# Centred values, unit keys in PSUM and a head norm cut in pieces, in a two-block kernel on one Trainium2 core

## The chip, the cores and the metric

The kernel runs on one core of one Trainium2 chip. The metric is the device time of one execution in microseconds (us), the median of several runs. It was 1239.25 us before the change (3 runs, 1236.81 to 1241.57).

## The reference, cut to what matters

512 tokens of width 1024 pass an RWKV-7 layer, a differential attention layer and then a second block (short convolution and stick-breaking attention). The change touches the RWKV layer alone, up to the first tiles of its output projection. `rh`, `wh`, `kh`, `vh` and `ah` are r, the decay, k, v and a, split into 16 heads of 64:

```python
kk = (k * k_k).reshape(B, S, H, N)
kk = kk / jnp.maximum(jnp.sqrt(jnp.sum(kk * kk, axis=-1, keepdims=True)), 1e-12)
k = k * (1.0 + (a - 1.0) * k_a)
bh = kk * ah
def step(state, inp):
    r_t, w_t, k_t, v_t, kk_t, b_t = inp
    sa = jnp.einsum('bhij,bhj->bhi', state, kk_t)
    state = (state * w_t[:, :, None, :] - sa[..., None] * b_t[:, :, None, :]
             + v_t[..., None] * k_t[:, :, None, :])
    return state, jnp.einsum('bhij,bhj->bhi', state, r_t)
mean = jnp.mean(y, axis=-1, keepdims=True)
var = jnp.mean(jnp.square(y - mean), axis=-1, keepdims=True)
y = (y - mean) * lax.rsqrt(var + GN_EPS) * ln_w + ln_b
bonus = jnp.sum(rh * kh * r_k, axis=-1, keepdims=True) * vh
return ((y + bonus) * jax.nn.silu(gate)) @ w_out
```

## The kernel before, in words

Activations lie as 8 tiles of 128 channels by 512 tokens (`NT` is 8, `TOK` is 512). A large product runs in **slots** of one output tile each: 24 matmuls of 128x512, three for each of 8 input tiles, because every fp32 number is split into a high and a low part (`split_product`, L639). ScalarE makes a slot's high weights (`hi`, L1310), GpSimd its low weights (`low_part`, L558, two subtractions of 128x512), both in two buffers, so `hi` of a slot waits for the product two slots back. Each engine runs one long program in the order in which it is written by hand, and semaphores tie them together. A wait at the head of an engine's queue holds up all that stands behind it.

The RWKV layer has these phases.

**Key and receptance runs** (8 slots each, L781 to L838). In the receptance run VectorE works through one key tile after another (`elements`, L2046; `receptance`, L2064; `bonus_mul`, L2069) and adds the token mix of the value run (`mix_v`, L2075). `elements(j)` multiplies the key by the reciprocal norm of its head, which TensorE has spread from 32 rows to a bank (`kk_spread`, L798, `head_spread`, L734). The unit key is kept in SBUF (`T1`, L2044). `kk_spread(j)` waits for the first instruction of `elements(j-1)` only (L802). The rows of reciprocal norms are first parted into a high and a low part for the fast fp32r product: L1472 on ScalarE, L2042 on VectorE. TensorE's order in an iteration is slot, `kk_spread(j+1)`, then `block_a(j-1)` (L805), whose 32 products are sent to DRAM.

**Value and gate runs** (L853 to L871). After each value slot `turn_v` (L840) turns a value tile with four transposes and `bonus_spread` spreads the bonus rows. VectorE meanwhile inverts 64x64 triangular problems in 30 steps (L2121). The steps stand in one order with `bonus(j)` (L2109) and with `lo_mix` (L1985), the low parts of the gate run's input, whose high parts are ScalarE's (`split_mix`, L1386). ScalarE also stacks the turned values (`stack_v`, L1527) and writes the bonus to DRAM (`bonus_out`, L1535).

**Chunk loop** (`NC` is 8, L993 to L1014). The turned blocks leave through `TURNED` (L274, L2153) and come back by DMA. For each chunk of 64 tokens TensorE runs `w_of`, `u_of`, `y_state`, `s_of`, `y_chunk`, while GpSimd places keys and values (L575 to L591) and scales the state, and ScalarE keeps y (`keep_y`, L1607).

**Head norm** (L1016 to L1037). Only when all of y is there, 8 matmuls subtract the mean of each head (L1030), ScalarE squares (L1644), TensorE sums over heads (L731), ScalarE takes the root and VectorE parts it (L2235). TensorE spreads it (L1037), and VectorE scales, adds the bonus and splits tile after tile (L2291 to L2301) for the first slot of the output projection. The first residual tile is L2251.

```python
        for k in range(NT):
            if k + 4 < NT:
                gated_bonus(k + 4)
            if k + 2 < NT:
                gn_scale(k + 2)
            if k + 1 < NT:
                gn_add(k + 1)
            split_lo(A_RWO, 0, k, YT[:, k, :])
```

SyncE's queue issues the weights and most other loads in order (L375 to L509). The bonus comes back in one load of 2 MB behind the last y (L505 to L507).

Of the kernel before, what the change touches and what calls it, by code (L numbers as in the profile page):

```python
# [25 lines left out]
P = 128  # L26
# [35 lines left out]
for _name, _w in (("ident", P), ("ones", P), ("center", P), ("causal_add", P), ("strict_add", P),  # L62
                  ("strict_s", CH), ("incl_s", CH), ("head_pick", 2 * BL),
                  ("pick", 2 * BL), ("eps", 6)):
    CONST_COLS[_name] = (_at, _at + _w)
    _at += _w
# [3 lines left out]
def constant_tables():  # L70
# [13 lines left out]
    eps = np.concatenate([eps, np.where(low_part, -1.0, 1.0)[:, None], low_part[:, None]], axis=1)  # L84
# [93 lines left out]
def gn_tile_bank(j):  # L178

    return (0, 1, 2, 3, 4, 5, 7, 0)[j]  # L180


# [10 lines left out]
def emit(nc, ctx, a, out):  # L193
# [60 lines left out]
    def over(start, entries):  # L254
# [19 lines left out]
    (TURNED,) = phase([("turned", [P, BL * BL])], tail_at + BL * BL * 4)  # L274
# [7 lines left out]
    BVT, SPREADH2, SPREADHR2, RK2, RKS2, RKC2 = phase([  # L282
        ("bonus_v", [P, NT, TOK]), ("spread_heads2", [P, 2, P]), ("spread_heads2_r", [P, 2, P], F32R),
        ("gn_rstd", [P, TOK]), ("gn_signed", [P, TOK], F32R), ("gn_parts", [P, TOK], F32R)])

    (GSQ,) = phase([("gn_squares", [P, NT, TOK])], 2 * FULL)
# [42 lines left out]
    def gn_bank(j):  # L329
        return BANK[gn_tile_bank(j)]  # L330
# [45 lines left out]
    def _(sp):  # L376
# [125 lines left out]

        sp.wait_ge(sem("v_placed"), 2 * 2 * NC)
        sp.dma_start(XT[:, :, :], D_XT.rearrange("j p t -> p j t")).then_inc(sem("x_spilled"), 16)
        sp.wait_ge(sem("y_even"), 2 * NC)  # L505
        sp.wait_ge(sem("y_odd"), 2 * NC)
        sp.dma_start(BVT[:, :, :], D_BV.rearrange("j p t -> p j t")).then_inc(sem("gn_in"), 16)  # L507
        sp.dma_start(SPREADH2[:, :, :], a["spread_heads"]).then_inc(sem("gn_in"), 16)
# [48 lines left out]
    def _(pool):  # L557
# [45 lines left out]

        def scale_state(c):
# [5 lines left out]
        for par in range(2):  # L610
            pool.wait_ge(sem(f"a_out{par}"), 16 * 4 * (NT // 2))
        scale_nk(0)
# [6 lines left out]
        pool.wait_ge(sem("prob_in"), 48)  # L619
        place_v(in_uv, 1)  # L620
        for c in range(NC - 1):
            if c:
                scale_state(c)
            place_kt(c + 1)
            place_v(in_sv(c + 1), 2 * c + 2)
            if c == 0:
                low_part(RUN_RWO[0], 1)
# [3 lines left out]
            place_v(in_uv, 2 * c + 3)  # L631
        for u in range(2, 4):
# [5 lines left out]
    def _(pe):  # L638
# [188 lines left out]
        for j in range(NT):  # L827
# [3 lines left out]
            else:  # L831
                rw_slot(NT + j, (lambda: kk_spread(NT - 1)) if j == NT - 1 else None)
# [7 lines left out]
        def turn_v(j):  # L840
# [3 lines left out]
            turn_four(BANK[6 - 2 * (j % 2)], [TMP[:, j % 2, t * P:(t + 1) * P] for t in range(TT)]).then_inc(sem("v_turn_mm"), 1)  # L844
# [8 lines left out]
        for j in range(NT):  # L853
# [3 lines left out]
            if j == 1:  # L857
                bonus_sums(1)
                pe.wait_ge(sem("kk_unit"), NT)
# [101 lines left out]
        def y_at(h, j):  # L961

            return YB[h][(low, up)[(h + j) % 2]][:, tile_cols(j)]

        def y_state(c):
            if c:
                pe.wait_ge(sem("y_even"), 2 * c)
                pe.wait_ge(sem("y_odd"), 2 * c)
            else:
                pe.wait_ge(sem("x_kept"), 8)  # L970
            for j in range(NT):
                for h, hp in enumerate((low, up)):
                    pe.matmul(y_at(h, j), SVX[c % 2][hp, j, h, :], KRX[hp, 1, j, chunk(c)], start=(j < 2), stop=False,
                              skip_group_check=True)

        def y_chunk(c):
# [3 lines left out]
            for j in range(NT):  # L980
                for h in ((0, 1), (1, 0))[j % 2]:
                    m = pe.matmul(y_at(h, j), UV[:, j, h, :], XR[:, c % 2, j, h, :], start=False, stop=(j >= NT - 2),
                                  skip_group_check=True)
            m.then_inc(sem("yx_mm"), 1)

# [7 lines left out]
        for c in range(NC):  # L993
            more = c + 1 < NC
            w_of(c)
            if c == 0:
# [6 lines left out]
            y_state(c)  # L1003
# [11 lines left out]

        pe.wait_ge(sem("y_even"), 2 * NC)  # L1016
        pe.wait_ge(sem("y_odd"), 2 * NC)
        center = cst("center")

        def gn_sums(b):  # L1020
            pe.wait_ge(sem("gn_squared"), 4 * b + 4)
            for j in range(4 * b, 4 * b + 4):
                m = head_sum(BANK[6], GSQ[:, j, :], j)
# [1632 lines left out]
```

## Time and profile before

| what | value |
|---|---|
| median of 3 runs | 1239.25 us (1236.81 to 1241.57) |
| the profiled execution | 1243.05 us |
| its span | 1241.3 us |
| busy in the span | PE 1161.3 (94%), DVE 753.1 (61%), ACT 619.9 (50%), POOL 486.4 (39%) |
| receptance run | about 120 to 190 us of the span |
| value and gate runs | about 184 to 287 us |
| chunk loop | about 287 to 370 us |
| head norm, to the first residual tile | about 370 to 408 us |

PE is TensorE, PEld its weight loads, DVE VectorE, ACT ScalarE, POOL GpSimd, SP SyncE. Times in rows count from the start of the span. A row of a timeline gives the start, the time of the group, the engine, the line, the operation with output and inputs, the number of instructions and, in brackets, how long the engine had been idle and what it waited for. The profiled execution is 3.80 us longer than the median.

### The profile page before, as it was taken

The numbers are of one execution on the slowest core, as the hardware profiler recorded it, in microseconds if no ns is written. First come the engines' busy times: TensorE is split into PE (matmuls) and PEld (weight loads), VectorE is DVE, ScalarE is ACT, GpSimd is POOL, SyncE is SP. The second block draws the span as 40 slices with busy tenths as digits, with TensorE's granted clock in tenths as the row PEclk, the third lists the DMA queues.
The fourth block names the chain that finished last, engine by engine and source line by source line (L and its number), as shares of the span: only waits on it lengthen the run. The fifth ranks groups of instructions, "written<-read, shape, count | busy, mean of one in ns | idle before, by whom it ended". The sixth has DMA issues, their size and how long they took to land.

```text
span 1241.3 us, 19538 instructions
## 1 busy us (share of the span) xinstructions
PE 1161.3 (94%) x7570; PEld 897.6 (72%) x7570; DVE 753.1 (61%) x1179; ACT 619.9 (50%) x1034; POOL 486.4 (39%) x391
## 2 busy tenths in 40 slices
PE   5899899998886999899999998999999999999987
PEld 5666667787772787677777776877888888867766
DVE  4775997895458436466666655374285234657773
ACT  4666453634553446566556464364221244556655
POOL 1333334357650344333323343443444445532231
PEclk8999899999997899899999999999999999999999
DMA  7742244526213253212222222522333333322111
GB/s 237 248 123 63 58 119 122 166 87 159 51 60 117 67 179 88 83 52 69 68 69 68 68 69 71 166 85 76 95 102 88 99 102 92 95 68 69 51 35 68
DMA packets 198941, 119.49 MB, mean 96 GB/s; under 512 B 27773, under 2 KB 187206, under 8 KB 198598
## 3 DMA queue, kind: packets, MB, share of 16 engines
q1 hardware_dynamic: 196256, 115.95, 32.1%
q10 hardware_dynamic: 2598, 2.33, 0.6%
q8 instruction: 60, 0.98, 0.3%
q14 instruction: 27, 0.22, 0.1%
HBM read 103.06 MB, written 15.20 MB: 95 GB/s over the span
## 4 chain that ended last, share of the span: by engine, by line
PE 41%; issue 30%; POOL 13%; DVE 12%; ACT 2%; DMA 1%; POOLq 0%; SPq 0%; ACTq 0%; DVEq 0%
POOL b_w_lo L562 13%; PE banks L643 10%; PE banks L645 10%; PE banks L644 10%; DVE b_problems L2127 1%; DVE b_sum_squares L2125 1%; PE banks L1218 1%; DVE b_a_lo L1987 1%; PE banks L650 1%; PE banks L891 1%; DVE b_suffix L2576 1%; PE banks L1246 1%; PE banks L910 1%; PE banks L1030 1%; DVE b_sum_squares L2060 1%
## 5 line engine op out<-in xcount | busy, mean ns | idle before, releaser
L562 POOL TENSOR_TENSOR b_w_lo<-b_w_raw,b_w_hi 128x512 fp32r<-128x512 f32 x320 | 430.4, 1366 | 710.7 <-ACT b_w_hi L1316 710.5
L643 PE MATMUL banks<-b_a_lo,b_w_hi 128*128 128x512 f32 x1280 | 524.9, 410 | 24.2 <-DVE b_a_lo L2243 8.6
L645 PE MATMUL banks<-b_a_hi,b_w_lo 128*128 128x512 f32 x1280 | 505.9, 395 | 0.0
L644 PE MATMUL banks<-b_a_hi,b_w_hi 128*128 128x512 f32 x1280 | 505.3, 395 | 0.0
L643 PEld LDWEIGHTS banks<-b_a_lo,b_w_hi 128*128 128x128 f32 x1280 | 244.1, 191 | 103.4 <-issue 21.6
L1316 ACT ACTIVATE b_w_hi<-b_w_raw 128x1024 fp32r<-128x1024 f32 x160 | 168.8, 1055 | 248.3 <-PE banks L645 242.9
L645 PEld LDWEIGHTS banks<-b_a_hi,b_w_lo 128*128 128x128 f32 x1280 | 244.0, 191 | 54.0
L644 PEld LDWEIGHTS banks<-b_a_hi,b_w_hi 128*128 128x128 f32 x1280 | 244.5, 191 | 44.5
L1723 ACT ACTIVATE b_exps<-banks,b_stats 128x128 f32<-128x128 f32 (+3 forms) x64 | 33.2, 524 | 61.3 <-DVE b_stats L2366 61.3
L1657 ACT ACTIVATE b_a_hi<-b_x_t,b_params 128x512 fp32r<-128x512 f32 x48 | 34.0, 719 | 55.5 <-DVE b_x_t L2251 54.9
L2251 DVE TENSOR_TENSOR b_x_t<-b_x_t,banks 128x512 f32<-128x512 f32 x32 | 22.0, 687 | 60.8 <-PE banks L645 60.8
L2364 DVE TENSOR_TENSOR banks<-banks,b_consts 128x256 f32<-128x256 f32 x32 | 13.9, 433 | 50.4 <-PE banks L1097 49.0
L2245 DVE SCALAR_TENSOR_TENSOR b_a_lo<-b_x_t,b_params,b_a_hi 128x512 fp32r<-128x512 f32 x32 | 30.1, 954 | 21.3 <-ACT b_a_hi L1657 21.3
L1710 ACT ACTIVATE b_rope_tmp<-banks 32x512 f32<-32x512 f32 x64 | 37.7, 588 | 3.0 <-DVE b_dq_t L2340 2.1
L1125 PEld LDWEIGHTS banks<-b_att_t,b_dv_rows 128*128 128x128 f32 x160 | 20.3, 190 | 14.5 <-issue 13.6
L1097 PE MATMUL banks<-b_dk_t,b_dq_t 64*128 64x128 f32 (+3 forms) x128 | 26.2, 487 | 4.7 <-DVE b_dk_t L2340 4.7
L2572 DVE TENSOR_TENSOR_SCAN b_suffix<-b_consts,b_softplus 128x512 f32<-128x512 f32 (+3 forms) x32 | 29.4, 919 | 1.1
L2365 DVE TENSOR_REDUCE b_stats<-banks 128x2 f32<-128x256 f32 (+3 forms) x32 | 26.4, 825 | 1.1
L1125 PE MATMUL banks<-b_att_t,b_dv_rows 128*128 128x128 f32 x160 | 26.2, 295 | 0.0
L2283 DVE TENSOR_TENSOR banks<-banks,b_rstd 128x512 f32<-128x512 f32 x16 | 11.2, 698 | 24.6 <-PE banks L645 18.1
L2484 DVE TENSOR_TENSOR b_conv_u<-banks,b_rstd 128x512 f32<-128x512 f32 x8 | 5.5, 692 | 32.0 <-PE banks L645 27.8
L2127 DVE TENSOR_TENSOR b_problems<-b_problems,b_sum_squares 128x60 f32<-128x60 f32 (+14 forms) x30 | 23.1, 771 | 1.0
(314 smaller groups left out, 1508.6 us busy)
## 6 DMA issues: line engine op xcount, KB each, us to landing
b_w_raw<-rw_w_in SPq DMA_DIRECT2D x32, 512.0 KB, 4.3
b_w_raw<-da_w_in SPq DMA_DIRECT2D x32, 512.0 KB, 4.0
b_w_raw<-w_in_a SPq DMA_DIRECT2D x32, 512.0 KB, 4.0
b_w_raw<-pe_w_gate SPq DMA_DIRECT2D x16, 512.0 KB, 4.1
d_ple<-b_ple_out SPq DMA_DIRECT2D x16, 256.0 KB, 4.8
b_w_raw<-rw_w_out SPq DMA_DIRECT2D x8, 512.0 KB, 4.6
b_ple_in<-d_ple SPq DMA_DIRECT2D x2, 2048.0 KB, 10.2
b_w_raw<-da_w_out SPq DMA_DIRECT2D x8, 512.0 KB, 4.1
```

The costliest lines, as they stand in the source:

```text
L562: m = pool.tensor_tensor(WLO[:, u % 2, ks], WRAW[:, u, ks], WHI[:, u % 2, ks].bitcast(F32), ALU.subtract)
L643: pe.matmul(dst, hi, a_lo[:, k_act, :], start=first, stop=False)
L644: pe.matmul(dst, hi, a_hi[:, k_act, :], start=False, stop=False)
L645: return pe.matmul(dst, lo, a_hi[:, k_act, :], start=False, stop=last)
L1125: m = pe.matmul(BANK[7][:, q * P:(q + 1) * P], DV[:, t, j * P:(j + 1) * P], ATTT[:, s % 2, t * P:(t + 1) * P], start=(t == 0), stop=(t == q))
L1316: act.activation(WHI[:, g % 2], WRAW[:, g % 4], ACT.Copy).then_inc(sem("hi_done"), 1)
L1657: m = act.activation(ACTS[buf][0][:, k, :], src, ACT.Identity, scale=scale)
L1710: m = act.activation(RTMP[32 * (q ^ 1):32 * (q ^ 1) + 32, 0, :], BANK[(3 * j + which) % 3][32 * q:32 * q + 32, :], ACT.Copy)
L1723: act.activation(ES[:, s % 2, comp, 0:w], PS[:, 3 + comp, 0:w], ACT.Exp, bias=STAT[:, s % 2, 2 + comp:3 + comp], scale=QK_SCALE, accum_out ...
L2127: own.step(tt(blk[:, :, 0:n, n + 1:BL], blk[:, :, 0:n, n + 1:BL], outer, ALU.add))
L2245: m = stt(out=a_lo[:, k, :], in0=src, scalar=scale, in1=a_hi[:, k, :].bitcast(F32), op0=ALU.mult, op1=ALU.subtract)
L2572: own.step(dve.tensor_tensor_scan(suf[:, h, ::-1], ONES[:, 0:1].to_broadcast([P, w]), sp[:, h, ::-1], 0.0, ALU.mult, ALU.add))
```

## The change

All of it lies in the RWKV layer:

- **Unit keys in PSUM.** `T1` becomes bank 6, where the spread norms lie. `kk_spread(j)` therefore waits for the whole of `elements(j-1)`. The parted rows are gone: ScalarE writes the reciprocal roots (with a factor of 4 under the root, since each head's row stands twice) and the spread is one plain fp32 matmul. The last column of each decay chunk (`PC`) is computed by ScalarE instead of copied by VectorE.
- **Two value mixes** (tiles 0 and 1) are made before the scans, not in the receptance loop.
- **Centred values.** `turn_v` multiplies by the centring matrix in place of the identity, so that y has mean zero in each head. The 8 centring matmuls of the head norm are gone.
- **Turned blocks** lie in a weight buffer, `WRAW[:, 2]`. GpSimd's first `place_v(in_uv, 1)` no longer waits for the problems' DMA. `place_v(in_sv(1))` and the first state do.
- **Head norm in pieces.** Columns 0 to 383 of y are squared on ScalarE and summed on TensorE in the last two chunks, columns 384 to 447 and 448 to 511 after them. The last chunk's y goes to banks 0 and 1, and VectorE keeps half of it. `ln_b` is added by ScalarE in `bonus_out`, GpSimd multiplies the bonus of tiles 0 to 3 and 4 by the gate in the chunk loop, VectorE multiplies y of tiles 0 to 4 by the gate ahead. The norm's scaling, adding and gating are done in PSUM, and the spreads of tiles 4 to 7 stand among the products of the first output slot.

```diff
-    (TURNED,) = phase([("turned", [P, BL * BL])], tail_at + BL * BL * 4)
+    TURNED = WRAW[:, 2].rearrange("p k n -> p (k n)")
+    PREGATED = 5
+    GN_SPLIT = (NC - 2) * CH
...
+        sp.wait_ge(sem("u_mm"), 4)
+        for j in range(4):
+            load_bonus(j)
+        sp.wait_ge(sem("u_mm"), 6)
+        for j in range(4, 6):
+            load_bonus(j)
+        sp.wait_ge(sem("s_mm"), 6)
+        for j in range(6, NT):
+            load_bonus(j)
...
-        sp.dma_start(BVT[:, :, :], D_BV.rearrange("j p t -> p j t")).then_inc(sem("gn_in"), 16)
...
-        pool.wait_ge(sem("prob_in"), 48)
+        pool.wait_ge(sem("bonus_v"), NT)
         place_v(in_uv, 1)
...
             place_v(in_sv(c + 1), 2 * c + 2)
+            if c == NC - 3:
+                for j in range(3):
+                    gate_bonus(j)
+            if c == NC - 2:
+                gate_bonus(3)
...
         def kk_spread(j):
             if j == 0:
-                pe.wait_ge(sem("kk_rstd"), 4)
+                pe.wait_ge(sem("kk_rstd"), 2)
             else:
-                pe.wait_ge(sem("kk_unit"), j)
-            head_spread(BANK[6], SPREADHR, RKC, j).then_inc(sem("kk_bcast"), 1)
+                pe.wait_ge(sem("el_done"), j)
+            head_spread(BANK[6], SPREADH, ACC, j).then_inc(sem("kk_bcast"), 1)
...
-            turn_four(BANK[6 - 2 * (j % 2)], [TMP[:, j % 2, t * P:(t + 1) * P] for t in range(TT)]).then_inc(sem("v_turn_mm"), 1)
+            bank = BANK[6 - 2 * (j % 2)]
+            for t in range(TT):
+                m = pe.matmul(bank[:, t * P:(t + 1) * P], TMP[:, j % 2, t * P:(t + 1) * P], cst("center"), start=(t == 0),
+                              stop=(t == TT - 1), skip_group_check=True)
+            m.then_inc(sem("v_turn_mm"), 1)
...
             w_of(c)
+            if c == NC - 1:
+                y_state(c)
+                gn_sums(slice(0, GN_SPLIT), 4, range(4))
...
-            y_state(c)
+            if more:
+                y_state(c)
+            else:
+                gn_sums(slice(0, GN_SPLIT), NT, range(4, NT))
...
+        gn_sums(slice(GN_SPLIT, GN_SPLIT + CH), NT + 1)
...
+        gn_sums(slice(GN_SPLIT + CH, TOK), NT + 2)
...
+        def first_out_slot():
+
+            pe.wait_ge(sem("lo_done"), RUN_RWO[0] + 1)
+            pe.wait_ge(sem("bank_free"), RUN_RWO[1] - 3)
+            for k in range(NT):
+                pe.wait_ge(sem("act_ready"), A_RWO + k + 1)
+                last = split_product(BANK[0], RUN_RWO[0] % 2, lambda w, k=k: w[:, k, :], k, k == 0, k == NT - 1, 0)
+                if k + 4 < NT:
+                    gn_spread(k + 4)
+            last.then_inc(sem("mm_done"), 1)
...
-        act.activation(RKS[:, :], RK, ACT.Identity, scale=SIGN).then_inc(sem("kk_rstd"), 1)
+        own.step(act.activation(RK, RK, ACT.Ln, scale=4.0))
+        act.activation(ACC[:, :], RK, ACT.Exp, scale=-0.5).then_inc(sem("kk_rstd"), 1)
...
         def bonus_out(j):
             act.wait_ge(sem("bonus_v"), j + 1)
+            own.step(act.activation(TMP[:, 2 + j % 2, :], TMP[:, 2 + j % 2, :], ACT.Identity, bias=prm(LN_B, j)))
...
+            if c == NC - 2:
+                act.wait_ge(sem("x_mm"), 2 * NC)
...
+                for j in range(NT):
+                    gn_square(slice(0, GN_SPLIT), j)
...
-        T1, T3 = ACC[:, :], RB[:, :]
+        T1, T3 = BANK[6], RB[:, :]
...
+            if j >= 2:
+                mix_v(j)
...
-            if k + 4 < NT:
-                gated_bonus(k + 4)
             if k + 2 < NT:
                 gn_scale(k + 2)
             if k + 1 < NT:
                 gn_add(k + 1)
-            split_lo(A_RWO, 0, k, YT[:, k, :])
+            split_lo(A_RWO, 0, k, BANK[4 + k % 4])
+            if PREGATED <= k + 1 < NT:
+                gn_gate(k + 1)
```

## Rows read from the trace of the kernel before

**Rows 1.** The page's chain that ended last, share of the span by engine.

```profile
PE 41%; issue 30%; POOL 13%; DVE 12%; ACT 2%; DMA 1%; POOLq 0%; SPq 0%; ACTq 0%; DVEq 0%
```

**Rows 2.** Timeline of ScalarE, then VectorE, before the first spread.

```profile
124.53 0.72 ACT L1472 ACTIVATE b_head_signed<-b_sigmoids,b_consts 128x512 fp32r<-128x512 f32 x1
...
125.28 0.75 DVE L2042 SCALAR_TENSOR_TENSOR b_head_parts<-b_sigmoids,b_consts,b_head_signed 128x512 fp32r<-128x512 f32 x1 [2.11 <-ACT b_head_signed L1472]
```

**Rows 3.** Timeline of VectorE in the receptance run.

```profile
143.30 0.74 DVE L2051 SCALAR_TENSOR_TENSOR b_sum_squares<-b_kt_rt,b_params,banks 128x512 f32<-128x512 f32 x1
...
145.35 1.27 DVE L2058 COPY b_kt_rt<-b_sum_squares 128x8 f32<-128x8 f32 x1
...
146.65 1.73 DVE L2060 SCALAR_TENSOR_TENSOR b_sum_squares<-b_sum_squares,b_nb_kh 128x512 f32<-128x512 f32 x1
...
178.52 0.74 DVE L2051 SCALAR_TENSOR_TENSOR b_sum_squares<-b_kt_rt,b_params,banks 128x512 f32<-128x512 f32 x1
...
183.82 6.48 DVE L1987 TENSOR_TENSOR b_a_lo<-b_mix_v,b_a_hi 128x512 fp32r<-128x512 f32 x7
```

**Rows 4.** Timeline of GpSimd, then VectorE, where the two overlap.

```profile
144.85 2.98 POOL L562 TENSOR_TENSOR b_w_lo<-b_w_raw,b_w_hi 128x512 fp32r<-128x512 f32 x2 [4.07 <-ACT b_w_hi L1316]
...
241.43 2.65 POOL L562 TENSOR_TENSOR b_w_lo<-b_w_raw,b_w_hi 128x512 fp32r<-128x512 f32 x2 [4.59 <-ACT b_w_hi L1316]
...
241.60 0.68 DVE L2114 TENSOR_TENSOR b_rw_tmp<-b_rw_tmp,banks 128x512 f32<-128x512 f32 x1
```

**Rows 5.** Timeline of TensorE in the receptance run.

```profile
128.21 0.80 PE L643 MATMUL banks<-b_a_lo,b_w_hi 128*128 128x512 f32 x1
...
136.25 0.49 PE L738 MATMUL banks<-b_head_parts,b_spread_heads_r 32*128 32x512 f32 x1
...
136.67 0.69 PE L815 MATMUL banks<-b_kt_rt,b_nb_kh 64*64 64x64 f32 x32
...
137.30 0.50 PE L643 MATMUL banks<-b_a_lo,b_w_hi 128*128 128x512 f32 x1
```

**Rows 6.** Windows: busy PE, PEld, DVE, ACT, POOL (instructions), PE clock, DMA share, GB/s.

```profile
124.00:128.00 4.00, 1.34 (x4) 0.46 (x2) 2.06 (x4) 3.97 (x8) 0.00 (x0) 0.81 0.17 52
...
128.00:132.00 4.00, 4.00 (x10) 3.02 (x10) 3.90 (x6) 0.98 (x2) 2.94 (x2) 0.50 0.02 4
```

**Rows 7.** Timeline of TensorE: plain fp32 products elsewhere.

```profile
104.24 1.13 PE L772 MATMUL banks<-b_lora_t,b_lora_w 64*128 64x512 f32 x4
...
1079.66 1.16 PE L663 MATMUL banks<-b_consts,b_params 128*128 128x128 f32 x8 [0.85 <-DVE b_params L1958]
```

**Rows 8.** Timeline of TensorE, ScalarE and VectorE, end of the value run.

```profile
232.51 0.60 PE L650 MATMUL banks<-b_consts,b_rw_tmp 128*128 128x128 f32 x4
...
239.03 0.60 PE L650 MATMUL banks<-b_consts,b_rw_tmp 128*128 128x128 f32 x4
...
239.55 0.49 PE L738 MATMUL banks<-b_head_parts,b_spread_heads_r 32*128 32x512 f32 x1
...
236.66 3.75 ACT L1395 ACTIVATE b_a_hi<-b_h_t 128x512 fp32r<-128x512 f32 x7
...
245.16 0.69 DVE L1987 TENSOR_TENSOR b_a_lo<-b_h_t,b_a_hi 128x512 fp32r<-128x512 f32 x1 [2.88 <-ACT b_a_hi L1395]
```

**Rows 9.** Timeline of TensorE, the first work on the turned blocks.

```profile
290.15 1.20 PE L925 MATMUL banks<-b_blocks_turned,b_blocks 32*32 32x32 f32 x64 [0.57 <-DMA b_blocks<-d_t]
```

**Rows 10.** Timeline of ScalarE, TensorE and VectorE in the head norm.

```profile
370.15 1.58 ACT L1582 ACTIVATE b_y_t<-banks 64x256 f32<-64x256 f32 x4 [1.37 <-PE banks L982]
...
371.88 7.94 PE L1030 MATMUL banks<-b_y_t,b_consts 128*128 128x512 f32 x14 [1.76 <-ACT b_y_t L1582]
...
387.24 0.80 PE L738 MATMUL banks<-b_gn_parts,b_spread_heads_r 32*128 32x512 f32 x4 [3.62 <-DVE b_gn_parts L2235]
...
388.04 1.28 DVE L2225 TENSOR_TENSOR b_y_t<-b_y_t,banks 128x512 f32<-128x512 f32 x2 [0.94 <-PE banks L738]
...
408.26 0.69 DVE L2251 TENSOR_TENSOR b_x_t<-b_x_t,banks 128x512 f32<-128x512 f32 x1 [2.38 <-PE banks L645]
```

More of the change, by code:

```diff
@@ L831, in _ @@
             else:
-                rw_slot(NT + j, (lambda: kk_spread(NT - 1)) if j == NT - 1 else None)
+                rw_slot(NT + j)
+            if j == NT - 1:
+                kk_spread(j)
             if j < NT - 2:
@@ L981, in y_chunk, with gn_sums @@
                 for h in ((0, 1), (1, 0))[j % 2]:
-                    m = pe.matmul(y_at(h, j), UV[:, j, h, :], XR[:, c % 2, j, h, :], start=False, stop=(j >= NT - 2),
+                    m = pe.matmul(y_at(c, h, j), UV[:, j, h, :], XR[:, c % 2, j, h, :], start=False, stop=(j >= NT - 2),
                                   skip_group_check=True)
             m.then_inc(sem("yx_mm"), 1)
+        def gn_sums(cols, squares, tiles=range(NT)):
+            pe.wait_ge(sem("rows_kept"), 6 * (NC - 1))
+            pe.wait_ge(sem("gn_squared"), squares)
+            for j in tiles:
+                m = head_sum(BANK[2][:, cols], GSQ[:, j, cols], j)
+            m.then_inc(sem("gn_mm"), 1)
         for g in range(2):
@@ L1058, in run_of @@
                 whole_slot(run, j, a0, buf, norm[1] if norm is not None and j == 1 else None)
-        run_of(RUN_RWO, A_RWO, 0)
+        first_out_slot()
+        for j in range(1, NT):
+            whole_slot(RUN_RWO, j, A_RWO, 0)
         run_of(RUN_PE0, A_PE0, 1, norm=norm_rows(16, 4))
@@ L1605, in keep_second_corner, with gn_square @@
             keep(dst[:, :, :, BL:CH], BANK[4 - h][block_rows(h, 0)].rearrange("p (n j t) -> p n j t", j=NT, t=BL), "corner_kept")
+        def gn_square(dst_cols, tiles):
+            act.activation(GSQ[:, tiles, dst_cols], YT[:, tiles, dst_cols], ACT.Square).then_inc(sem("gn_squared"), 1)
         def keep_y(c):
             act.wait_ge(sem("yx_mm"), c + 1)
-            for h, done in enumerate(("y_even", "y_odd")):
+            for h, done in enumerate(("y_even", "y_odd")[:1 if c == NC - 1 else 2]):
                 for par in range(2):
-                    src = BANK[6 + h][(low, up)[(h + par) % 2]].rearrange("p (j e t) -> p e j t", e=2, t=CH)
+                    src = BANK[h if c == NC - 1 else 6 + h][(low, up)[(h + par) % 2]].rearrange("p (j e t) -> p e j t", e=2, t=CH)
                     keep(YT[(low, up)[h], par::2, c * CH:(c + 1) * CH], src[:, par], done)
@@ L2017, in _ @@
             mixed(NKX[:, 1, k, :], MU_R, k).then_inc(sem("mix_done"), 1)
+        for j in range(2):
+            mix_v(j)
         dve.wait_ge(sem("tables_in"), 32)
@@ L2188, in keep, with gate_product @@
             dve.tensor_copy(dst, src).then_inc(sem(done), 1)
+        def gate_product(j, cols):
+            dve.wait_ge(sem("gn_squared"), j + 1 if cols.stop == GN_SPLIT else NT + 2)
+            own.step(stt(out=YT[:, j, cols], in0=YT[:, j, cols], scalar=prm(LN_W, j), in1=GT[:, j, cols], op0=ALU.mult, op1=ALU.mult))
         for g in range(2):
@@ L2205, in _ @@
                 keep_incl(c + 1, 0)
-            dve.wait_ge(sem("u_mm"), c + 1)
+            if c < NC - 1:
+                dve.wait_ge(sem("u_mm"), c + 1)
             if c == 0:
                 dve.wait_ge(sem("v_placed"), 4)
+            if c == NC - 1:
+                gate_product(0, slice(0, GN_SPLIT))
+                gate_product(1, slice(0, GN_SPLIT))
+                dve.wait_ge(sem("u_mm"), c + 1)
             keep(UV[up, :, 1, :], tiles(BANK[3][up]), "u_kept")
+            if c == NC - 1:
+                for j in range(2, PREGATED):
+                    gate_product(j, slice(0, GN_SPLIT))
             if c + 1 < NC:
```

147 lines of the change are left out of this document (75 added, 72 removed).

## The prediction, made before the changed kernel was run

> **What bounds the kernel now.** I read the page's chain first: TensorE has 41% of it, waits that the profile cannot name 30%, GpSimd 13%, VectorE 12% [rows 1]. That is an average. The change touches 120 to 408 us only, so I followed the timelines there.
>
> In the receptance run VectorE is the bound. From the first instruction of `elements(2)` at 143.30 to that of `elements(6)` at 178.52 its timeline has no gap: 35.2 us for four tiles, two extra mixes and one extra receptance (2.0 us together), so 8.3 a tile. The reader should see which durations are odd there: a copy of 8 columns takes 1.27 us, a 512-column multiplication 1.73 instead of 0.74 [rows 3], just while GpSimd makes low weights from 144.85 on [rows 4]. Each of GpSimd's two subtractions holds one such instruction up by about 1.05 us, 2.1 a tile. Undisturbed, a tile is 6.2. The multiplication at 241.60 reads one operand from a bank, lies wholly under GpSimd's row of 241.43, and takes 0.68 [rows 4].
>
> In the value run TensorE works without a gap, one slot in 6.52 us (232.51 to 239.03), of which 0.52 is `turn_v` and 0.42 the spread [rows 5, 8], so 5.58 is the slot. After it VectorE's inversion stands behind the last `lo_mix`, which at 245.16 had waited 2.88 for ScalarE [rows 8]. It ends the phase, through a DMA wait at 290.15 [rows 9]. In the head norm nothing overlaps: y is kept at 370.15, centring runs 7.94 us, the spreads start at 387.24, VectorE's tile loop at 388.04, and the first residual tile comes at 408.26, 2.38 after VectorE fell idle [rows 10].
>
> **The sum, part by part.** Negative is faster.
>
> *Start of the receptance run.* The parting of rows leaves the chain: 0.72 on ScalarE and 0.75 on VectorE, 124.53 to 126.03 [rows 2]. A plain fp32 spread comes in for a fast one. Two such products side by side take 1.13, with 1.06 to the next slot [rows 7], so I take 0.96 for one, against 0.42 between the starts of 136.25 and 136.67 [rows 5]. `elements(0)` starts 1.0 earlier. The bounds are -1.5 and -0.4.
>
> *The wait for all of `elements`.* `kk_spread(1)` now waits until `elements(0)` ends, near 131, not 127.5. Slot 9 is queued behind it, and its products are what receptance(1) needs. TensorE had already idled here: it was busy 1.34 of 4 us, and the granted clock went to 0.50 (1.2 GHz) in the next window [rows 6]. Slot 9 took 8.0 us at mixed clocks, 128.21 to 136.25 [rows 5]. After a longer idle I let it run 3.6 us at half speed again. It ends at 139.9, 3.7 later than before. The bounds are +1 and +6.
>
> *The pace after that.* TensorE needs slot 5.58, spread 0.96 and `block_a` 0.63 (136.67 to 137.30 [rows 5]), 7.2 a tile. VectorE loses the small copy and, with `T1` in a bank, most instructions with two SBUF inputs. Four are left (K times PI, the last product, mix and bonus). I give them one stall: 6.1 + 1.05 = 7.2. Both are at 7.2 against 8.3. Slot 14 ends at 139.9 + 5 x 7.2 + 1.0 (bonus sums) = 176.9. receptance(6), ahead of `elements(6)` on VectorE, waits for that, so `elements(6)` starts at 177.5 instead of 178.52 and, with one stall less, ends 1.6 before 183.82 [rows 3]. The value run starts its low parts **1.5 earlier**. The pace is worth 6 us and TensorE's new order takes most of it back. The two mixes ahead fill a VectorE that later waits for sigmoids, so cost nothing. With that cover gone they cost 2 x 0.74. ScalarE's small exponentials replace a copy, on an engine busy 0.98 of 4 us in its window [rows 6].
>
> Here a page of the Trainium skill bears. "SBUF — State Buffer", section "Who interferes with whom", says that a VectorE instruction with two SBUF inputs contends with a GpSimd instruction that reads SBUF, that one with at most one SBUF input does not, and that the loser waits. By that rule, the trace agrees (1.73 and 0.68 above). The same rule speaks against the full gain, since four such instructions stay.
>
> *The value run.* `turn_v` becomes four real fp32 products of 128 columns. The nearest row is four of that shape from 1079.66, 0.92 to the next matmul [rows 7], against 0.52: +0.4. Six of them lie before the last value slot has fed the gate run: **+2.4**. The bounds are 0 and +4.
>
> *`ln_b` on ScalarE.* An extra 128x512 instruction, 0.72 as in [rows 2], and a wait for it. Queued behind it are the splits of the gate run: once ahead of the seven splits from 236.66, once between `stack_v(5)` and the last split, for which the `lo_mix` at 245.16 waits [rows 8]. That puts two on the path: **+1.5**, bounds 0 and +1.7. Less 0.4 of slack in the first: net +1.1. The bonus DMA leaves some 2.4 us later, hidden in the 6.5 of a slot.
>
> So the chunk loop starts 1.5 earlier, then later by 2.4 and 1.1: **+2.0**. The new wait before `TURNED` is for a gate slot's low weights, done some 5 us before, and costs nothing.
>
> *The chunk loop.* GpSimd's placing of values is freed from a DMA. TensorE's wait there is not named by the trace, so 0, bounds -2.8 and 0. The bonus now comes during the loop, 2 MB in 8 loads, on SyncE's queue behind the turned blocks and ahead of x and the next weights. I take 0, bounds 0 and +3: TensorE's own instructions come by DMA too. GpSimd's gate products, 1.3 to 1.5 each [rows 4], are three ahead of one `place_v`; the same engine has a gap of 3 us at that point. Cost 0, at worst +1.3.
>
> *The head norm.* Half the sums of 384 columns and `y_state` stand ahead of the last `u_of`: +0.5, so y is ready at 370.65. VectorE finishes three gate products first, then copies its half: 372.0. Square 0.65, short sums 0.6, two ScalarE steps of 0.7: 374.65. The four spreads take 0.80 at half speed now [rows 10]. Plain fp32 doubles that: 376.4. VectorE's loop starts at **376.4 instead of 388.04**. It has 27 instructions at 0.61 (8 scale, 8 add, 8 low, 3 gate) for 28 before: 16.5. The last two low parts wait for ScalarE, +1.0. Spreads 4 to 7 stand in TensorE's queue behind products that wait for low parts. The first two at half speed are late by 2.2 together. End 396.1, then three products: residual at 397.2 against 408.26, **-11.0**. Bounds: -12.5 without late spreads, -7.5 if the clock stays at 0.50 (3.0 a tile on TensorE for 1.8 on VectorE).
>
> *Sum:* +2.0 - 11.0 = **-9.0**. The profiled execution's own 1243.05 would become 1234.05. It stands 3.80 above the median, so the median 1239.25 becomes **1230.3**. No later phase reads anything that moved, so I let the gain pass through.
>
> **The rivals.** A change under 0.5% (6.2 us) cannot be told from none by a measurement of this kernel.
>
> *A: the sum,* 0.38, own range 1226 to 1233.
>
> *B: the receptance run gains more,* 0.22. `elements(0)` has no stall and the clock comes back sooner, so slot 9 ends near 136.5 and both remaining terms shrink: 3.5 more. 1226.8. For it: GpSimd's pair falls within 3 us of a slot's end, where few two-input instructions stand. Against: the waits of the old order show only with TensorE already late.
>
> *C: the norm's loop becomes TensorE's,* 0.18. The clock stays at 0.50 and the norm gives -7.5: 1233.8. For it: TensorE has little to do between 370 and 380 now too, and the spreads from 387.24 take 0.80 instead of 0.5.
>
> *D: the stalls stay,* 0.13. Both of GpSimd's subtractions find a two-input instruction in each tile. The pace stays 8.3, costing 6 x 1.1 = 6.6: 1236.9. It is the same rule of the Trainium skill ("SBUF — State Buffer", "Who interferes with whom") taken to its end.
>
> *E: slower,* 0.09. The place is `kk_spread(j+1)`'s new wait. If `elements` ends about 2 us after the slot, TensorE idles and its clock falls again, as [rows 6] show after one idle. A slot at half speed costs 24 x 0.2 = 4.7 more. From three such slots on it decides: -9.0 + 14.1 = +5.1, 1244.4. Against it, my estimate has `elements` 0.5 us ahead of the slot.
>
> **How the numbers follow.** The forecast is A's 1230.3. The range 1223.5 to 1240 takes in B with the lower bounds, C and D, and leaves E and the ends out. Faster by over 0.5% means under 1233.05: A nearly whole, B, a third of C, 0.65. Slower over 1245.4: half of E and some sums of upper bounds, 0.08. Within: 0.27.
>
> **What would show it.** `elements(6)` should start near 177.5 and value slots be 6.9 apart. The turned blocks should be used near 292. Then VectorE's first scaling should follow the last y products by 6 us, not 18, and the first residual tile come 27 us after them, not 38. The 8-column copy should be short wherever it stands. I am wrong if TensorE's clock is 0.50 in several windows of 140 to 180, if nameless waits grow in the chunk loop, or if the low weights, not the norm, end the first output slots.

## The result, and the profile of the changed kernel

The changed kernel took 1246.62 us, the median of 13 runs (1243.35 to 1247.92), beside 1241.6 us for the kernel before (13 runs, 1236.81 to 1244.3). The ratio is 1.0045, 95% interval 1.0032 to 1.0059: 0.3 to 0.6% slower, where 1230.3 and a gain had been forecast. The profiled execution took 1247.3, its span is 1245.5, 4.2 longer than the span before.

The chain of the page, shares of the span by engine, answers to [rows 1]:

```profile
PE 47%; issue 29%; POOL 13%; DVE 6%; ACT 3%; DMA 1%; POOLq 0%; ACTq 0%; DVEq 0%
```

VectorE's share has halved, as the change wants, and TensorE has taken all of it. The DMAs have 1% as before, but new among the lines of the chain is the bonus on its way to DRAM (`d_bonus_v`, 1%). To see where the time went, I cut the way from the start of the receptance run to the end at events that both kernels have, and took the times between them from the timelines:

| from ... to | before | changed | difference |
|---|---|---|---|
| VectorE's first instruction on RK (122.48; 123.90) ... first low part of the value run (183.82; 184.96) | 61.3 | 61.1 | -0.3 |
| ... last low part for the gate run (245.16; 251.60) | 61.3 | 66.6 | +5.3 |
| ... first x_a of the chunk loop (288.19; 297.81) | 43.0 | 46.2 | +3.2 |
| ... last y kept by ScalarE (370.15; 378.53) | 82.0 | 80.7 | -1.2 |
| ... first residual tile (408.26; 411.19) | 38.1 | 32.7 | -5.4 |

These add up to +1.5. Another 1.4 was there before the changed code began: VectorE's mixes near 55 us met GpSimd in other places and GpSimd's low weights at 61.83 came at 63.26. The executions of one kernel differ by more than that. After the first residual tile 1.3 more appear, 0.7 of them in the next tile. So the head norm gave half of its 11 us and the value and gate runs took 8.5 where 3.5 was forecast.

**The receptance run.** VectorE's timeline, against [rows 3]:

```profile
131.67 0.68 DVE L2124 TENSOR_TENSOR b_kt_rt<-banks,b_rw_tmp 128x512 f32<-128x512 f32 x1
...
141.42 0.69 DVE L2124 TENSOR_TENSOR b_kt_rt<-banks,b_rw_tmp 128x512 f32<-128x512 f32 x1 [3.30 <-PE banks L667]
...
143.47 1.14 DVE L2112 TENSOR_TENSOR b_nb_kh<-b_kt_rt,b_rw_tmp 128x512 f32<-128x512 f32 x1
...
148.76 0.69 DVE L2124 TENSOR_TENSOR b_kt_rt<-banks,b_rw_tmp 128x512 f32<-128x512 f32 x1 [0.64 <-PE banks L667]
```

L2124 is `receptance`. The second one waits 3.30 for slot 9, the next three 0.64 or 0.65, and they follow each other at 7.35: TensorE sets the pace. From the third tile to the sixth one instruction a tile meets GpSimd and takes 1.14 instead of 0.68.

**The value run.** The chain of waits in order of time, up to the third `bonus` (224.03) and on to the fourth (232.00); only its longest pieces are shown (columns: start, us, what the chain ran through):

```profile
219.69 0.62 ACT b_rw_tmp L1581
220.33 3.58 DMA d_bonus_v<-b_rw_tmp
224.03 0.70 DVE b_rw_tmp L2169
224.83 0.60 ACT b_rw_tmp L1567
226.66 0.38 ACT b_v_stack L1577
227.05 0.62 ACT b_rw_tmp L1581
227.69 4.19 DMA d_bonus_v<-b_rw_tmp
232.00 0.70 DVE b_rw_tmp L2169
```

The reader should see a ring: the Identity that adds `ln_b` (L1581), its DMA, `bonus` on VectorE (L2169), which must not write the buffer before the DMA has read it, `keep_v` on ScalarE (L1567), `stack_v` (L1577), the next Identity. It takes 7.97 us a tile here (224.03 to 232.00), and TensorE needs 7.03. The three waits on the DMA are 1.82, 3.18 and 1.22. At the end of the phase VectorE waits 4.06 for ScalarE before the last low part (2.88 before the change), and TensorE stands. VectorE and TensorE:

```profile
251.60 0.69 DVE L2046 TENSOR_TENSOR b_a_lo<-b_h_t,b_a_hi 128x512 fp32r<-128x512 f32 x1 [4.06 <-ACT b_a_hi L1440]
```

```profile
252.35 0.50 PE L665 MATMUL banks<-b_a_lo,b_w_hi 128*128 128x512 f32 x1 [2.72 <-DVE b_a_lo L2046]
...
253.15 1.31 PE L870 MATMUL banks<-b_consts,b_rw_tmp 128*128 128x128 f32 x8
254.39 0.79 PE L760 MATMUL banks<-b_head_parts,b_spread_heads_r 32*128 32x512 f32 x1
```

After this idle of 2.72 (0.88 before the change) TensorE's granted clock falls (the window 250 to 260 shows 0.69), the gate run ends later than the inverse, and the first x_a waits 11.34 for TensorE where it had waited 6.17.

**The head norm.** VectorE's loop starts 6.8 us after the last y and not 17.9, much as forecast (about 6). Then TensorE's timeline, against [rows 10]:

```profile
383.14 2.09 PE L760 MATMUL banks<-b_gn_rstd,b_spread_heads 32*128 32x512 f32 x8 [1.55 <-ACT b_gn_rstd L1706]
389.12 0.76 PE L665 MATMUL banks<-b_a_lo,b_w_hi 128*128 128x512 f32 x1 [3.88 <-DVE b_a_lo L2319]
...
390.66 2.07 PE L760 MATMUL banks<-b_gn_rstd,b_spread_heads 32*128 32x512 f32 x2
392.66 0.80 PE L665 MATMUL banks<-b_a_lo,b_w_hi 128*128 128x512 f32 x1
...
394.24 2.07 PE L760 MATMUL banks<-b_gn_rstd,b_spread_heads 32*128 32x512 f32 x2
```

One fp32 spread shows as two records (x2). So four spreads side by side take 2.09 us (x8), and one alone takes 2.07 (x2). The late four, one behind each block of the first output slot, make the loop TensorE's at 3.58 us a tile (390.66 to 394.24). The windows (columns as in [rows 6]) show its clock:

```profile
378.00:382.00 4.00, 1.51 (x49) 1.07 (x45) 3.04 (x8) 1.74 (x4) 0.00 (x0) 0.76 1.01 372
382.00:386.00 4.00, 2.09 (x8) 0.55 (x8) 1.41 (x4) 0.97 (x2) 0.00 (x0) 0.50 0.99 272
...
394.00:398.00 4.00, 4.00 (x7) 1.51 (x7) 2.31 (x5) 0.86 (x2) 0.00 (x0) 0.50 0.00 0
```

### The profile page after: what moved, and what is told of

Read it like the earlier page. It is cut to its first block, busy times and chain, and to the rows that moved or that the text cites. A ratio compares the mean times of both kernels' runs of the same rounds, so it can differ in the third digit from the quotient of the medians.

```text
span 1245.5 us, 19707 instructions
## 1 busy us (share of the span) xinstructions
PE 1175.8 (94%) x7634; PEld 906.5 (73%) x7634; DVE 736.4 (59%) x1168; ACT 622.6 (50%) x1047; POOL 492.2 (40%) x396
## 4 chain that ended last, share of the span: by engine, by line
PE 47%; issue 29%; POOL 13%; DVE 6%; ACT 3%; DMA 1%; POOLq 0%; ACTq 0%; DVEq 0%
POOL b_w_lo L570 13%; PE banks L665 12%; PE banks L667 11%; PE banks L666 11%; PE banks L760 2%; PE banks L1263 1%; DVE b_a_lo L2046 1%; PE banks L919 1%; PE banks L672 1%; DVE b_suffix L2652 1%; PE banks L1291 1%; DMA d_bonus_v<-b_rw_tmp 1%; PE banks L938 1%; PE banks L1273 1%; PE banks L985 1%
## 5 line engine op out<-in xcount | busy, mean ns | idle before, releaser
L2223 DVE TENSOR_TENSOR b_x_a<-banks,b_consts 64x256 f32<-64x256 f32 x32 | 13.5, 422 | 20.5 <-PE banks L920 20.0
```

## The experiments

My theory: the loss is the ring in the value run and the late spreads in the norm; the receptance part gives nothing, since slot 9 waits for `elements`. The main rival: the fp32 turn, or the two parts' meeting, costs the time. All ratios are to the kernel before, run beside each. Its own median lay between 1239.47 and 1241.6 in the five sets of runs, so differences of medians between two changed kernels carry that much doubt where they come from different sets.

**e1: no Identity in `bonus_out`.**

```diff
-            own.step(act.activation(TMP[:, 2 + j % 2, :], TMP[:, 2 + j % 2, :], ACT.Identity, bias=prm(LN_B, j)))
```

> The changed kernel without the Identity that adds ln_b in bonus_out (this kernel leaves ln_b out of the result). Theory: the Identity stands behind the four copies of stack_v, so each bonus DMA leaves about 5 us later than before, VectorE's bonus waits for it (1.82, 3.18, 1.22 us at bonus(2) to bonus(4)), and ScalarE's next keep_v waits for bonus: a ring of 7 to 8 us a tile. Then all waits of bonus on d_bonus_v vanish, the last lo_mix of the gate run comes near 247 instead of 251.60, TensorE keeps its clock between 250 and 260, VectorE's first x_a comes near 290 instead of 297.81, and the kernel takes 5 to 8 us less than the changed one (1239 to 1242). Rival: the four fp32 products of turn_v set the value run; then only the two steps on the path go, 1 to 2 us less (1245).

Measured: 1242.48, ratio 1.0017 (1.0004 to 1.003), 4.1 less than the changed kernel by the medians and 3.5 by the ratios, where the theory had 5 to 8. No `bonus` waits for a DMA. VectorE's last low part and first x_a:

```profile
249.17 0.69 DVE L2045 TENSOR_TENSOR b_a_lo<-b_h_t,b_a_hi 128x512 fp32r<-128x512 f32 x1 [2.88 <-ACT b_a_hi L1440]
...
292.64 1.78 DVE L2222 TENSOR_TENSOR b_x_a<-banks,b_consts 64x256 f32<-64x256 f32 x4 [6.17 <-PE banks L920]
```

The waits are those of before again (2.88 and 6.17), and the phase ends 5.2 earlier. From the first value low part to the last gate one it is 64.25 us, against 66.64 with the Identity and 61.34 before. So the Identity costs 2.4 up to there and 2.7 behind it, and 2.9 is left for the turn. The rival (1 to 2 us) falls.

**e2: seven spreads ahead of the first output slot.** Tiles 4 to 6 go to banks 1 to 3, which are free then.

```diff
+def gn_bank(j):
+    return (4, 5, 6, 7, 1, 2, 3, 4)[j]
...
-            z = BANK[4 + j % 4]
+            z = BANK[gn_bank(j)]
...
-        for j in range(4):
+        for j in range(7):
             gn_spread(j)
...
-                if k + 4 < NT:
-                    gn_spread(k + 4)
+                if k == 0:
+                    gn_spread(7)
```

> The changed kernel with the norm's tiles 4 to 6 in banks 1 to 3, so that seven spreads are issued ahead of the first output slot and only the last one within it. Theory: a plain fp32 spread alone takes 2.07 us at half clock, four side by side 2.09, so the late ones at one per product make the loop TensorE's (3.58 us a tile). Then VectorE's waits on the spread (2.01, 1.69, 1.63, 1.03) vanish but for one, the first residual tile comes 27 us after the last y product instead of 32.7, and the time falls by 5 to 6.5 us (1240 to 1241.5). Rival: the loop is bound by the round of scale, add, hi, lo between VectorE and ScalarE; then the waits move to ScalarE and the time falls by under 1.5 us.

Measured: 1239.45, ratio 0.9989 (0.9971 to 1.0007), 7.2 less than the changed kernel, a little more than the theory's 5 to 6.5. The first residual tile comes 25.9 after the last y, not 32.7. TensorE:

```profile
383.17 3.79 PE L765 MATMUL banks<-b_gn_rstd,b_spread_heads 32*128 32x512 f32 x14 [1.55 <-ACT b_gn_rstd L1711]
```

Seven spreads in 3.79, with VectorE already at work on the first: the late waits on spreads (2.01, 1.69, 1.63, 1.03) are gone, and from 385.32 VectorE's only gap is one of 0.66 for the last tile's copy on ScalarE. The rival falls.

**e3 and e4: each half alone.** The receptance hunks of the diff on the kernel before (unit keys in bank 6, fp32 spread, two mixes, chunk decays on ScalarE), and all the others without them.

```diff
+            head_spread(BANK[6], SPREADH, ACC, j).then_inc(sem("kk_bcast"), 1)
...
+        T1, T3 = BANK[6], RB[:, :]
```

> The kernel before with the receptance part of the change alone (unit keys in a bank, plain fp32 spread, two value mixes ahead, the wait for all of elements, chunk decays on ScalarE). Theory: the run is now TensorE's at 7.35 a tile after a slot 9 that ends near 141, so the value run starts 0.3 to 1 us earlier and the kernel takes 0 to 1 us less than the one before. Rival 1, what was forecast: 1.5 less. Rival 2: the slower clock of 130 to 140 costs more than the shorter start gives, 1 to 2 us more than before.

> The kernel before with the rest of the change alone (centred turn, ln_b on ScalarE, turned blocks in the weight buffer, head norm from banks), the receptance run as it was. Theory: all of the loss is here, so it takes as long as the changed kernel or up to 1 us more, 1246 to 1248, with the same waits of bonus on its DMA. Rival: the loss needs both parts (the new place of the receptance run's GpSimd work or its clock); then it is within 2 us of the kernel before.

Measured: e3 1240.37, ratio 1.0002 (0.9988 to 1.0017); e4 1246.5, ratio 1.0023 (0.9995 to 1.0052, five runs). Up to the value run's low parts e3 takes 61.2 us and e4 61.5, against 61.3 before: the receptance part is worth nothing. The interval of e4 includes 1, so its time alone decides nothing; its profile has the changed kernel's waits of `bonus` on the DMA (2.99, 3.08, 1.35), and its last gate low part 66.8 after the first value one. By these the loss does not need both halves. TensorE and VectorE in e3:

```profile
129.08 2.07 PE L739 MATMUL banks<-b_sum_squares,b_spread_heads 32*128 32x512 f32 x2 [4.71 <-DVE b_nb_kh L2065]
```

```profile
138.82 0.69 DVE L2070 TENSOR_TENSOR b_kt_rt<-banks,b_rw_tmp 128x512 f32<-128x512 f32 x1 [3.42 <-PE banks L646]
```

TensorE stands 4.71 for `elements(0)`, then spreads at half clock, then starts slot 9.

**e5: the spread in the middle of the slot.** On e3's kernel.

```diff
-                rw_slot(NT + j)
+                rw_slot(NT + j, (lambda j=j: kk_spread(j)) if j < NT - 1 else None)
...
-            if j < NT - 2:
-                kk_spread(j + 1)
```

> The receptance part alone on the kernel before, with kk_spread(j) in the middle of slot 8 + j instead of ahead of it, so that TensorE doesn't stand at the end of elements while a slot's products wait behind the spread. Theory: the receptance part gave nothing (1240.4) because slot 9 waits for elements(0): TensorE stands 4.71 us at 124 to 129, its spread takes 2.07 at half clock, and VectorE's receptance(1) waits 3.42. Then slot 9 starts where it did before, that wait goes, and the value run's low parts come 58 us after the first instruction on RK instead of 61.2: 3 us less, 1237.5. Rival: VectorE's elements, not TensorE, hold the run as before; then the spread in the slot only makes elements later and the time stays at 1240 or rises by 1.

Measured: 1235.77, ratio 0.9968 (0.9951 to 0.9986), 4.6 less than e3 by the medians and 4.2 by the ratios, where 3 was forecast. The run takes 58.3 instead of 61.2. TensorE:

```profile
129.76 1.12 PE L739 MATMUL banks<-b_sum_squares,b_spread_heads 32*128 32x512 f32 x2 [1.75 <-DVE b_nb_kh L2063]
```

It stands 1.75 instead of 4.71, half of slot 9 is done before that, and the spread runs at full clock. So the idea of unit keys in a bank is good; the place of the wait took it away.

**e6: `bonus_out` ahead of `stack_v`.** On the changed kernel, with the Identity.

```diff
+            if j >= 3:
+                bonus_out(j - 3)
             if j >= 2:
                 stack_v(j - 2)
-            if j >= 3:
-                bonus_out(j - 3)
```

> The changed kernel with bonus_out(j - 3) ahead of stack_v(j - 2) in ScalarE's order; the Identity stays. Theory of the ring: the loss in the value run is the place of the Identity and its DMA behind the four copies, not its 0.72 us. The DMA then leaves 1.6 us earlier, the waits of bonus on d_bonus_v shrink from 1.2 to 3.2 to under 1, the last lo_mix comes within 3 us of 249.2, and 2.5 to 4 us of the 4.1 that taking the Identity out gave come back: 1242.5 to 1244. Rival: it is ScalarE's own time on the path (two Identities ahead of the splits); then the order changes nothing, 1246 to 1247.

Measured: 1241.78, ratio 1.0022 (1.0003 to 1.004). The ring is open: no `bonus` waits for the DMA. But one number went the rival's way: the last gate low part is still 66.3 after the first value one, with waits of 1.50 and 3.87 for ScalarE, where e1 without the Identity has 64.3. Up to there the ring cost only 0.4, and ScalarE's own time 2.0. The rest of what came back lies behind it: the first x_a is 44.3 after that low part, not 46.2. TensorE stood 2.32 there, not 2.72, and its granted clock stayed at 1.00 in every window from 248 to 264, where the changed kernel's fell to 0.50 (256 to 260).

From the first value low part to the first x_a the new order thus gives back 2.3 of the 5.1 that e1 does. The medians give 4.8 and the ratios 2.9, but the profiled execution is the slowest of e6's ten. Both views hold a share, and how large each is stays open: the place closes the ring, and ScalarE's time stands ahead of the splits.

**e7: three repairs in one kernel.** e2, e5, and `ln_b` added on ScalarE to the loaded bonus (tiles 0 to 4) or in VectorE's addition (tiles 5 to 7).

```diff
+                stt(out=z, in0=z, scalar=prm(LN_B, j), in1=bonus_home(j), op0=ALU.add, op1=ALU.add).then_inc(sem("gn_added"), 1)
...
+            if c == NC - 3:
+                for j in range(PREGATED):
+                    act.wait_ge(sem(f"bonus_in{j // 4}"), 64)
+                    act.activation(bonus_home(j), bonus_home(j), ACT.Identity, bias=prm(LN_B, j)).then_inc(sem("bonus_based"), 1)
```

> The whole changed kernel with three repairs: seven spreads ahead of the first output slot, ln_b added on ScalarE to the loaded bonus in the chunk loop (five tiles) and by VectorE's addition itself (three tiles) instead of in bonus_out, and the unit key's spread in the middle of the slot. If the three effects add: 1246.6 - 7.2 - 4.1 - 3 = 1232.3, 0.7% less than the kernel before. Rival: five Identities in the chunk loop stand on its path, which costs 1 to 3 us of it (1233 to 1235); or the earlier value run ends in the wait for the inverse, which then sets the chunk loop's start as in the kernel before, 1235.

Measured: 1234.54, ratio 0.9961 (0.994 to 0.9982), 2.2 above the sum. The profile speaks for the first rival, with a larger price than it named: the loop takes 87.1 from the first x_a to the last y, 6.3 more than in the changed kernel. ScalarE:

```profile
355.14 3.17 ACT L1693 ACTIVATE b_blocks<-b_blocks,b_params 128x512 f32<-128x512 f32 x5
358.34 0.59 ACT L1629 ACTIVATE b_rstd<-banks 64x512 f32<-64x512 f32 x1
```

The keeping of w (L1629, 358.34) stood behind the five Identities.

**e9: the same five in ScalarE's gaps.** GpSimd's five products with the gate move behind them, two of them after the loop.

```diff
+            if c == NC - 3:
+                base(0)
             act.wait_ge(sem("u_mm"), c + 1)
...
+            if c == NC - 2:
+                base(3)
+                base(4)
```

> The kernel of e7 with its five Identities no longer in one block of 3.17 us in the chunk loop, but each where ScalarE was waiting (one before u of chunk 5 is kept, one before and one behind its first corners, two before the squares), and GpSimd's five products behind them, two of those after the loop. Theory: the block held up the keeping of w in the last chunks, so the loop took 87.1 us from the first x_a to the last y against 80.7 in the changed kernel. Then it takes 81 to 83 and the kernel 1229 to 1231. Rival: the loop's length varies by itself by that much between executions (80.2 to 82.0 so far in kernels with the same loop), or the Identities cost wherever they stand; then 1233 to 1235.

Measured: 1231.39, ratio 0.9931 (0.9909 to 0.9952). The loop takes 79.6, under the band that the theory gave; the end is just above what it said. The rival that the loop's length varies by itself falls: with e9's order it takes 80.8 and 80.3 in e11 and e12 below, with e7's 87.1 and 85.2 (e7, e8). Nothing is left out in this kernel, and it beats the kernel before by 0.7% and the changed one by 1.1%; from e7 its interval does not part it. One cost of the new order was not removed: while GpSimd multiplies the last two bonus tiles (367.67 to 370.48), three of VectorE's products with the gate take 3.68 us instead of 1.93, its copy of y comes later, and the first residual tile is 27.8 after the last y, against 25.9 in e2.

**e10: no work added to the loop; e6's order with e2 and e5.** The diff is the sum of theirs.

> The changed kernel with seven spreads ahead of the first output slot, the unit key's spread in the middle of the slot, and bonus_out (with its Identity) ahead of stack_v: nothing added in the chunk loop. If the three effects of e2, e5 and e6 add: 1246.6 - 7.2 - 3.7 - 4.8 = 1231. Rival: with the receptance run shorter the value run's waits grow by as much, and it stays at the 1234.5 of e7.

Measured: 1233.42, ratio 0.9929 (0.9899 to 0.9958), eight runs from 1227.0 to 1237.5. By the ratio it is as good as e9; its median lies between the two theories. Its first x_a waits 8.57 for TensorE, so the gate run, not the inverse, still sets the loop's start. TensorE stood 2.32 before the last low part as in e6, but here its clock fell (0.65 in 252 to 256).

**e8 and e12: the turn without centring.** On e7 and on e9. These two kernels leave the centring of the values out.

```diff
-            for t in range(TT):
-                m = pe.matmul(bank[:, t * P:(t + 1) * P], TMP[:, j % 2, t * P:(t + 1) * P], cst("center"), start=(t == 0),
-                              stop=(t == TT - 1), skip_group_check=True)
+            turn_four(BANK[6 - 2 * (j % 2)], [TMP[:, j % 2, t * P:(t + 1) * P] for t in range(TT)]).then_inc(sem("v_turn_mm"), 1)
```

> The kernel of e7 with turn_v by the old transposes, which leaves the centring of the values out of the computation. Theory: the fp32 products with the centring matrix cost 0.46 us more a value slot, 2.9 us up to the last lo_mix. Then value slots are 6.5 apart again instead of 7.03 and the time is 2.5 to 3 us under e7's. Rival: the wait that ends the phase is the solve's or GpSimd's, so a shorter value run gives under 1 us.

> The kernel of e9 with turn_v by the old transposes (the centring of the values left out), in more rounds, since e7 and e8 differed in their profiled executions (1235.01 and 1229.33) and not in their medians (1234.5 and 1234.6). Theory: the fp32 products cost 2.9 us up to the last lo_mix and that passes through to the end: 1228.5, ratio 0.9908 where e9 has 0.9931. Rival: what is saved there is lost before the chunk loop or in it; then the ratio is that of e9.

Measured: e8 1234.63, ratio 0.9958 (0.994 to 0.9976); e12 1229.64, ratio 0.9925 (0.9901 to 0.9949, six runs). The profiles agree with each other: 61.3 from the first value low part to the last gate one in both, against 64.3 in e7 and e9, and from there to the first x_a 43.1 and 43.4 against 43.5 in both. The centring costs 2.9 to 3.0 and that reaches the chunk loop. Whether it reaches the end is not settled: e8's 2.5 to 3 less did not come, the medians give 0 and 1.8, and the intervals of all four overlap.

**e11: TensorE kept busy in the norm.** On e9.

```diff
+                pe.matmul(BANK[3][:, 0:GN_SPLIT], cst("ident"), GSQ[:, 0, 0:GN_SPLIT], start=True, stop=True)
```

> The kernel of e9 with five products of 384 columns added whose results nobody reads, three in TensorE's gap after the last y products and two behind the last sums of squares. Theory: the granted clock is 0.50 in the norm because TensorE has little to do while y is kept and squared (1.5 of 4 us busy at 378 to 382 in the changed kernel). Then the first spreads take 1.12 instead of 2.09 us and the first residual tile comes 1 to 2 us sooner after the last y. Rival: the clock falls all the same or the added products only stand in the way; no change or 0.5 to 1 us more.

Measured: 1232.97, ratio 0.9946 (0.9923 to 0.9968), not to be told from e9. TensorE's spreads, then the windows:

```profile
374.20 1.99 PE L764 MATMUL banks<-b_gn_rstd,b_spread_heads 32*128 32x512 f32 x14
```

```profile
370.00:374.00 4.00, 2.31 (x22) 0.98 (x20) 3.04 (x8) 1.89 (x3) 0.00 (x0) 1.00 1.00 375
374.00:378.00 4.00, 2.13 (x15) 0.80 (x14) 2.61 (x6) 0.66 (x2) 0.00 (x0) 1.00 1.00 278
378.00:382.00 4.00, 2.77 (x5) 1.33 (x5) 4.00 (x8) 1.19 (x2) 0.00 (x0) 0.63 0.06 13
```

The clock stayed at 1.00 (2.4 GHz) up to 378 and seven spreads took 1.99, not 3.79. The first residual tile came 26.6 after the last y against 27.8 in e9, so the clock was worth 1.2 there. From the start of VectorE's loop to the residual tile both take 19.28: with the late spreads gone, VectorE sets that loop, and TensorE's clock, which falls again, is not its bound.

## Why the prediction was wrong, point by point

**The start and the wait for all of `elements`** came as worked out. `elements(0)` starts 3.30 after the first instruction on RK, 4.21 before (-0.9, forecast -1.0). No cost of the two mixes ahead shows: the first instruction on RK comes at 121.18 in e3, which has them, and at 124.63 in e4, which has not. With the early shift taken off, receptance(1) found slot 9 done at 140.0 (139.9 forecast). One stall a tile was left, of 0.45 rather than 1.05, and [rows 4] held: the instruction that takes 1.14 has two SBUF inputs. The pace was 7.35 for 7.2, because one fp32 spread alone takes 1.12, not the 0.96 that I read from [rows 7]. That 0.15 a tile, five times, makes most of the 1.2 between the forecast gain of 1.5 and the measured 0.3. Most of the rest is a stall of 1.1 that `elements(6)` kept (1.78 at 180.41) and that I had taken away: with the early shift off it starts at 178.3 (177.5 forecast) and takes 5.2, against 5.3 before. I had named the wait, sized it, and taken it as given; e5 shows that it alone held back 2.9 us in the profile and 4.6 in the medians.

**`turn_v`**: +2.4 forecast, +2.9 measured (e1 against before), +2.9 to +3.0 by e8 and e12. The slots are 7.03 apart, 6.9 forecast.

**`ln_b` on ScalarE is the step that failed.** I put +1.1, bounds 0 and +1.7, and wrote that the bonus DMA leaves "some 2.4 us later, hidden in the 6.5 of a slot". The 2.4 was near: it is issued 2.9 after `keep_v` starts (217.47, 220.33), and 0.1 after it without the Identity (217.41, 217.55 in e1). The cover was not there. The DMA took 3.6 and 4.2 us to land, and what waits for it is not something a slot later but `bonus`, for which ScalarE's next `keep_v` waits in turn. The trace of before hinted at it in a row that I had not opened:

```profile
220.64 0.69 DVE L2114 TENSOR_TENSOR b_rw_tmp<-b_rw_tmp,banks 128x512 f32<-128x512 f32 x1 [0.35 <-DMA d_bonus_v<-b_rw_tmp]
```

That `bonus` waited 0.35, until its DMA of 5.5 us had landed, at the same time as the spread that it also needs; this tile had no slack. The next two DMAs of before landed 2.7 and 3.6 ahead of their `bonus`. So the later issue alone does not close the ring. With the 2.0 that the third DMA of the changed kernel took, my estimate of a round is 5.8 (7.4 and 8.0 less what the first two took above that), under TensorE's 7.03. Why the first two took longer no run here shows.

The price of the Identity is 5.1 up to the first x_a (e1 against the changed kernel, from the first value low part) and 4.1 in the medians, for +1.1 forecast. By e6's profile 2.3 of the 5.1 are the ring, which I had put at nothing, and 2.8 are ScalarE's own time ahead of the splits, which I had sized at 1.1; by the medians the ring is nearly all of it. That a late last low part can also be followed by a lower clock of TensorE and hand the end of the phase to the gate run was in neither the sum nor a rival.

**The new wait before the turned blocks** cost 0.36 in the profile, off the path, since the gate run was later. **The chunk loop**, 82.0 before, took 80.1 to 81.0 in the profiles of the changed kernel, e1, e2, e4 and e6, and with the old loop 80.6 in e3 and 79.0 in e5. So its length differs as much between kernels with the same loop as by the change: 0 within that, as put.

**The head norm** up to VectorE's loop gave 11.1 (17.9 to 6.8), where 11.6 had been worked out. The loop gave back 5.7: 25.9 us from its start to the residual tile, where 20.8 was forecast and 20.2 had been before. Rival C named this cause, with 0.18. The failed term is the spread's size. I read "x4 0.80" in [rows 10] as 0.2 a spread, doubled the row for four in fp32 (1.6; the sum has 1.75), and let two late ones cost 2.2 together. But those four ran side by side: a single spread from split parts at half clock takes 0.79 (254.39 above; the window 254 to 256 shows 0.50), as long as four. The trace of before had such a row too, which I had not used: 0.79 for the one spread at 127.50, just where [rows 6] show the clock fall. So in fp32 one takes 2.07, and the four late ones 8.3. The Trainium skill, "TensorEngine Tiling (Array Packing)", section "Key Properties", says that different tiles of the array "can execute LdWeights and Matmul in parallel"; the trace agrees (2.09 for four, 2.07 for one). With one at 2.07 and three products of 0.43, C's 3.0 a tile would have been 3.4; 3.58 was measured.

**Rival E**, a TensorE that keeps dropping its clock in the receptance run, did not come: one idle, and windows of 1.00 from 140 to 190. (A slot at half speed is 24 x 0.2 = 4.8 there, not 4.7.) That the kernel was slower, as E had it, has another cause. The forecast's sign was lost in two places: about 4 us in the value and gate runs (5.1 for 1.1) and 5.1 in the norm's loop.

## What to carry to other kernels

Before an instruction is put between a buffer's last writer and its DMA, follow the buffer round to whoever writes it next, and look in the trace how long before that write the slowest of these DMAs lands. When a row says "x4", look for a row with x1 before dividing by four. And where a wait is put in front of a slot of work that does not need it, move the wait into the slot: that made a half of the change that was worth nothing worth 0.3% (e5 against e3), and with the other repairs a kernel slower by 0.45% into one faster by 0.7% (e9).

## What the runs showed of the hardware that I had not expected

Small products on different row groups of the array overlap fully: 2.09 us for four fp32 spreads at half clock, 2.07 for one. In e1 a DMA issue on ScalarE's queue ran ahead of the four copies that stand before it in the program, where it waited for none of ScalarE's own results: issued at 224.63, copies from 225.11. In the changed kernel, with the Identity to wait for, the copies start at 218.10 and the issue comes at 220.33. TensorE's idle of 2.32 us before the last low part of the gate run was followed by a fall of the clock in e10 (0.65 in 252 to 256) and by none in e6 (1.00). TensorE at 1.2 GHz in the norm cost little once its single spreads were gone: keeping it at 2.4 GHz through seven of them was worth 1.2 us in the profile and nothing in the medians.
